# Expert gate and up in one TensorE core: rows held and split weights streamed in three fp32r products, with down one block behind

## What is computed

```python
MOE_BLOCK = 128
def run_block(args):
    xb, e = args                                   # 128 rows of 1024, the block's expert
    hid = jax.nn.silu(xb @ w_gate[e]) * (xb @ w_up[e])   # 1024 x 512 each
    return hid @ w_down[e]                         # 512 x 1024
yb = lax.map(run_block, (buf.reshape(n_blocks, MOE_BLOCK, D), block_e)).reshape(n_rows, D)
```

## Time and profile before

| | us |
|---|---|
| median of 3 runs | 3437.43 |
| lowest and highest run | 3433.58, 3445.54 |
| the profiled execution's own time | 3432.71 |
| its span, first to last instruction | 3431.0 |
| TensorE busy in the span | 2979.0 (87%) |
| VectorE, ScalarE, GpSimd busy | 1231.0, 1004.2, 233.1 |
| mean granted TensorE clock | 0.901 of full |

### The profile page before, as it was taken

How to read it: one execution, slowest core, us unless ns; L and a number is a source line. 1 busy time by engine, 2 the same in 40 slices (tenths; PEclk the granted TensorE clock), 3 DMA queues, 4 the chain that set the end, 5 groups by cost and what they waited for, 6 DMA issues and landing times. The chain is left out here.

```text
span 3431.0 us, 41076 instructions
## 1 busy us (share of the span) xinstructions
PE 2979.0 (87%) x15738; PEld 2379.3 (69%) x15738; DVE 1231.0 (36%) x2668; ACT 1004.2 (29%) x1633; POOL 233.1 (7%) x281
## 2 busy tenths in 40 slices
PE   5999799896499999995599989999698878888877
PEld 4887566596499999995478857788697734444457
DVE  4444411222233333334412135333222224555542
ACT  4223211111133333332411112112222324444431
POOL 0000300000200000002001012201100000000000
PEclk9999899996699999998799979558799888999989
DMA  3110641121599999996433144112203100000021
GB/s 84 43 46 4 256 142 38 36 75 58 205 345 342 344 344 344 344 343 232 145 98 117 43 132 97 51 28 50 96 13 98 33 19 1 1 1 1 1 86 68
DMA packets 284590, 412.06 MB, mean 120 GB/s; under 512 B 73579, under 2 KB 167403, under 8 KB 284332
## 3 DMA queue, kind: packets, MB, share of 16 engines
q1 hardware_dynamic: 247328, 302.70, 27.2%
q0 software_dynamic: 21088, 73.42, 5.6%
q10 hardware_dynamic: 16044, 34.17, 2.7%
HBM read 334.89 MB, written 75.28 MB: 120 GB/s over the span
## 5 line engine op out<-in xcount | busy, mean ns | idle before, releaser
L1280 PE MATMUL ps<-moe_xT,moe_wg 128*128 128x128 f32 x2048 | 251.3, 276 | 1.0 <-DVE moe_xT L1328 1.0
L1280 PE MATMUL ps<-moe_xT,moe_wu 128*128 128x128 f32 x2048 | 249.8, 275 | 0.0
L1280 PEld LDWEIGHTS ps<-moe_xT,moe_wg 128*128 128x128 f32 x2048 | 242.9, 193 | 4.0 <-issue 1.4
L1280 PEld LDWEIGHTS ps<-moe_xT,moe_wu 128*128 128x128 f32 x2048 | 239.3, 192 | 0.0
L155 DVE TENSOR_TENSOR moe_wd_parts<-moe_wd,moe_wd_parts 128x1024 fp32r<-128x1024 f32 x128 | 148.5, 1220 | 114.1 <-ACT moe_wd_parts L1309 114.1
L1937 PE MATMUL ps<-att_qx,att_kx 65*128 65x256 f32 (+1 forms) x512 | 165.4, 465 | 7.0 <-DMA att_qx<-att_RR 7.0
L2442 PE MATMUL ps<-c_kT,c_q 96*128 96x512 f32 (+3 forms) x384 | 153.1, 508 | 1.2 <-ACT c_kT L2489 0.7
L2020 ACT ACTIVATE att_sT<-att_sT 128x512 f32<-128x512 f32 (+1 forms) x104 | 63.8, 614 | 286.9 <-DVE att_sT L2095 286.9
L2463 PE MATMUL ps<-lattn_pT,X 128*64 128x512 f32 (+3 forms) x384 | 144.2, 531 | 0.7 <-ACT lattn_pT L2516 0.7
L1937 PEld LDWEIGHTS ps<-att_qx,att_kx 65*128 65x128 f32 x512 | 124.4, 285 | 20.7 <-DMA att_qx<-att_RR 7.1
L148 PE MATMUL ps<-ab_h,abp_w 128*128 128x512 f32 x336 | 134.9, 401 | 3.5 <-DVE abp_w L155 3.5
(11 more groups left out here) (470 smaller groups left out, 6343.1 us busy)
## 6 DMA issues: line engine op xcount, KB each, us to landing
moe_wg<-in_w_e_gate_dram SPq DMA_DIRECT2D x128, 512.0 KB, 4.8
moe_wu<-in_w_e_up_dram SPq DMA_DIRECT2D x128, 512.0 KB, 4.7
moe_wd<-in_w_e_down_dram SPq DMA_DIRECT2D x128, 512.0 KB, 9.3
y_rows<-merge_zero POOLq DMA_DIRECT2D x49, 512.0 KB
y_rows<-moe_y ACTq DMA_DIRECT2D x32, 512.0 KB, 5.5
abp_raw<-in_ab_w_in_dram SPq DMA_DIRECT2D x22, 512.0 KB, 4.1
proj_w_raw<-in_w_in_dram SPq DMA_DIRECT2D x20, 512.0 KB, 4.1
merge_raw<-in_w_in_dram SPq DMA_DIRECT2D x16, 512.0 KB, 6.7
```

The source lines that it names most:

```text
L1280: mm = pe.matmul(ps[:, which, f * P:(f + 1) * P], w[:, k, f * P:(f + 1) * P], xT[:, k, :], start=(k == 0 and f == 0), stop=(k == KT - 1), ...
```

## The change

Gate, up and down all become three fp32r products with the rows (or hidden rows) stationary, and 512 columns of weights streamed. The result of gate and up then has the rows on the partitions, so the hidden rows have to be turned on TensorE ahead of down (`turn_hidden`), and the turned rows and turned hidden rows are split into high and low parts. All weights are split: ScalarE copies the landed chunk to a high tile, and VectorE writes the low part over the landed chunk itself (`split_tile` puts the raw and the low tile at one address). GpSimd makes two of the four low parts of down. A chunk's next load therefore waits until TensorE has used the chunk. Down of block j runs after gate and up of block j + 1; the first and last turns are written out ahead of the loop and behind it. Gate and up chunks are cut from memory in another way: a partition takes eight consecutive weight rows, two to a chunk, so each chunk reads 4 KB in every 16 KB; before, a chunk was 512 KB in one piece, in rows of 2 KB.

```diff
-                link(dve.tensor_copy(R["n_blocks"][:, :], pend[0:1, cur, EXPERTS - 1:EXPERTS]))
+                for i in range(3):
+                    link(dve.tensor_scalar(be[:, i:i + 1], pend[0:1, cur, EXPERTS - 1:EXPERTS], -float(i), None, ALU.add))
+                link(dve.tensor_copy(R["n_blocks"][:, :], be[:, 0:3]))
...
+        def split_tile(name, shape):
+            high, at = sc.sb(name + "_high", shape, F32R), aligned(nc.sbuf_base)
+            low = sc.sb(name + "_low", shape, F32R)
+            return high, low, nc.alloc_sbuf_tensor_at(f"moe_{name}_raw", shape, F32, offset=at)
...
-        wg_d = w_gate.rearrange("e (c k p) f -> (e c) p k f", p=P, k=2)
+        wg_d = w_gate.rearrange("e (p c k) f -> e p c (k f)", c=GC, k=2)
+        wu_d = w_up.rearrange("e (p c k) f -> e p c (k f)", c=GC, k=2)
+        wd_d = w_down.rearrange("e (c p) d -> e p c d", p=P)
+        xg_cols = xg[:, :].rearrange("t (p k) -> t k p", k=KT)
...
+                def load_down(b, e):
                     for f in range(FT):
-                        sp.wait_ge(wd_split, i * FT + f + 1)
+                        sp.wait_ge(d_used, b * FT + (f + 1))
...
+                with sp.Fori(0, loops) as j:
+                    e = expert_of(j + 2)
+                    load_gate(j + 2, e)
+                    load_up(j + 2, e)
+                    load_down(j + 1, expert_of(j + 1))
...
+                def low_down(b):
+                    for i in range(ON_POOL):
+                        f = FT - ON_POOL + i
+                        pool.wait_ge(d_high, b * FT + (f + 1))
+                        pool.tensor_tensor(wd[1][:, f, :], wd[2][:, f, :], wd[0][:, f, :].bitcast(F32), ALU.subtract).then_inc(d_split_pool, 1)
+                with pool.Fori(0, loops) as j:
+                    gather(j + 3)
+                    low_down(j + 1)
...
+                def gate_up(b, bank, w, split, used):
                     for c in range(GC):
-                        for which, w in enumerate((wg, wu)):
-                            pe.wait_ge(loaded[2 * c + which], i * 16 + 16)
-                                    mm = pe.matmul(ps[:, which, f * P:(f + 1) * P], w[:, k, f * P:(f + 1) * P], xT[:, k, :],
+                        pe.wait_ge(split, b * GC + (c + 1))
+                        for k in range(2):
+                            n = 2 * c + k
+                            mm = multiply_split(pe, ps[:, bank, :], (xT[:, 0, n, :], xT[:, 1, n, :]), (w[0][:, c, k, :], w[1][:, c, k, :]), n == 0, n == KT - 1)
+                        mm.then_inc(used, 1)
...
+                with pe.Fori(0, loops) as j:
+                    gate(j + 1)
+                    turn_hidden(j)
+                    up(j + 1)
+                    turn_x(j + 2)
+                    down(j)
...
+                def high(b, w, loaded, made, c):
+                    act.wait_ge(loaded[c], b * 16 + 16)
+                    act.activation(w[0][:, c], w[2][:, c], ACT.Copy).then_inc(made, 1)
+                def rows_high(b):
+                    act.wait_ge(x_turned, b + 2)
+                    act.wait_ge(u_used, b * GC + GC)
+                    for n in range(2):
+                        act.activation(xT[:, 0, 4 * n:4 * n + 4, :], ps[:, 4 + n, :].rearrange("p (k t) -> p k t", t=P), ACT.Copy).then_inc(x_high, 1)
...
+                def low(b, w, n, high, made, c):
+                    dve.wait_ge(high, b * n + (c + 1))
+                    low_part(dve, w[1][:, c], w[2][:, c], w[0][:, c]).then_inc(made, 1)
```

More of the change, by code:

```diff
@@ L1222, in experts @@
+        hT = sc.sb("hT", [P, 2, FT, P], F32R)
         y = sc.sb("y", [P, D])
[L1223 to L1226 removed]
@@ L1264, in _ @@
+                last, loops = blocks_less(pool, 1), blocks_less(pool, 2)
+                for b in range(3):
+                    gather(b)
+                low_down(0)
+                with pool.Fori(0, loops) as j:
+                    gather(j + 3)
+                    low_down(j + 1)
+                low_down(last)
             @block.tensor
             def _(pe):
[L1266 to L1269, removed]
@@ L1320, in _ @@
-                act.wait_ge(y_stored, nb * 16 + 16)
+                last, loops = blocks_less(act, 1), blocks_less(act, 2)
+                rows_high(0)
+                for c in range(GC):
+                    high(0, wg, g_loaded, g_high, c)
+                for c in range(GC):
+                    high(0, wu, u_loaded, u_high, c)
+                silu(0)
+                for c in range(GC):
+                    high(1, wg, g_loaded, g_high, c)
+                for c in range(GC):
+                    high(1, wu, u_loaded, u_high, c)
@@ new lines, in _ @@
+                rows_high(1)
+                for f in range(FT):
+                    high(0, wd, d_loaded, d_high, f)
+                with act.Fori(0, loops) as j:
+                    silu(j + 1)
+                    for c in range(GC):
+                        high(j + 2, wg, g_loaded, g_high, c)
+                    hidden_high(j)
+                    for c in range(GC):
+                        high(j + 2, wu, u_loaded, u_high, c)
+                    rows_high(j + 2)
+                    for f in range(FT):
+                        high(j + 1, wd, d_loaded, d_high, f)
+                    out(j)
@@ L1321, in _ @@
+                silu(last)
+                hidden_high(loops)
+                for f in range(FT):
+                    high(last, wd, d_loaded, d_high, f)
+                out(loops)
+                hidden_high(last)
+                out(last)
+                act.wait_ge(y_stored, last * 16 + 32)
                 act.sem_inc(settled_act, 1)
@@ new lines, in out @@
+                def out(b):
+                    dve.wait_ge(d_used, b * FT + 2 * FT)
+                    dve.wait_ge(y_stored, b * 16 + 16)
+                    dve.tensor_copy(y[:, HALF:D], ps[:, 3, :]).then_inc(y_dve, 1)
+                dve.sem_inc(y_dve, 1)
+                dve.sem_inc(x_low, 2)
+                dve.sem_inc(hid_ready, 1)
+                dve.sem_inc(h_low, 1)
+                last, loops = blocks_less(dve, 1), blocks_less(dve, 2)
+                rows_low(0)
+                for c in range(GC):
+                    low(0, wg, GC, g_high, g_split, c)
@@ new lines, in _ @@
+                for c in range(GC):
+                    low(0, wu, GC, u_high, u_split, c)
+                for c in range(GC):
+                    low(1, wg, GC, g_high, g_split, c)
+                hidden(0)
+                for c in range(GC):
+                    low(1, wu, GC, u_high, u_split, c)
+                rows_low(1)
+                for f in range(FT - ON_POOL):
+                    low(0, wd, FT, d_high, d_split, f)
+                with dve.Fori(0, loops) as j:
+                    for c in range(GC):
+                        low(j + 2, wg, GC, g_high, g_split, c)
+                    hidden_low(j)
+                    hidden(j + 1)
+                    for c in range(GC):
+                        low(j + 2, wu, GC, u_high, u_split, c)
+                    rows_low(j + 2)
+                    for f in range(FT - ON_POOL):
+                        low(j + 1, wd, FT, d_high, d_split, f)
+                    out(j)
@@ L1351, in combine @@
+                hidden_low(loops)
+                hidden(last)
+                for f in range(FT - ON_POOL):
+                    low(last, wd, FT, d_high, d_split, f)
+                out(loops)
+                hidden_low(last)
+                out(last)
 def combine(nc, K, R, y_dram):
```

203 lines of the change are left out of this document (113 added, 90 removed).

## The result

The changed kernel took 3500.14 us (median of 4 runs, 3482.21 to 3518.79), the kernel before 3435.51 (4 runs) beside it: ratio 1.0169, 95% interval 1.012 to 1.0218. It is slower by some 65 us, where 3405 was forecast, and outside the range. The profiled execution took 3502.45; all of what follows is read from it.

A forecast was written before the change was run, and what follows sets the result against it. Rings of waits through the single-buffered weight tiles, L + 15.3 with L = 4.7, were to set a 20.0 us period; the stage ends at 1559.0 instead of 1591.9, 32.9 us off 3437.4, so 3405 us, range 3368 to 3455.

The forecast's parts named there:

- TensorE's work: Expert stage: gate, up and down at 5.46 us each plus turning 0.91 and 0.46, 17.75 us a block against 21.33.
- The DMA floor: Expert stage: 7.34 MB a block moved at an assumed 400 GB/s, so at least 18.4 us a block.
- The second ring: From down's last product through its last chunk's load and ScalarE's list to the next down: L + 15.30 us.
- L: Time from a weight load's issue to its landing, taken as 4.7 us.
- which then waits twice a block, some 2.2 us in all: TensorE waits before gate for the rows' low part and before down for the hidden rows', some 2.2 us a block.
- TensorE whose clock falls because it pauses: Slower case in the expert stage, sharing a chance of 0.04 with a ring beyond 5.8 + 0.3.
- Two rings close over one block: Expert stage: one ring through the rows, one through ScalarE's list, both L + 15.3, giving a period of 20.0 us.
- down's ring: The second ring, through down's last chunk and ScalarE's list: L + 15.30 us.
- the ring through the rows: From up's last product through its last chunk, the rows' low parts, gate, turning and up: L + 15.25 us.
- break-even: Period of 21.1 us, or L = 5.8, at which the change gains nothing; rival of no change, chance 0.15.
- Slow pieces: Rival: gate and up loads, 4 KB pieces 16 KB apart, run slowly; at 320 GB/s 3492 us; chance 0.11.
- VectorE and GpSimd block each other: Rival: their low parts can't run together, delaying up to 2.36 us a block; period 22.4, time 3476; chance 0.07.

The follow-up runs named there:

- The fastest run: Changed kernel with a raw tile of its own for every weight chunk and hidden and input rows' parts moved ahead of the splits: 3351.4 us, ratio 0.9779.
- the run with the input parts earlier: Changed kernel with only the input rows' high and low parts moved ahead of the splits of up: 3495.0 us, ratio 1.018.
- the hidden parts earlier: Changed kernel with the turned hidden rows' copy and low part moved ahead of gate's four chunk copies and low parts: 3496.0 us, ratio 1.0193.

## Why the prediction was wrong

- **TensorE's work, 17.75 us a block: right.** With nothing in its way a block takes 17.9, TensorE busy 98.9% of it.
- **The DMA floor, 18.4 us at 400 GB/s: near, and a little too high.** The fastest run moves 410 GB/s over 300 us and has a period of 17.89, under that floor. The Trainium skill's 358 GB/s ("DMA: Bandwidth & Descriptors", Specifications) was the other reading; this run does not hold to it, with one core active.
- **The second ring, L + 15.30 with L = 4.7: the right ring, mis-sized.** In the block shown L is 5.33 (+0.63), down 7.24 in place of 5.46 (+1.78, of which 1.55 is the clock), the four low parts of gate 4.96 to the start of the next in place of 4.64 (+0.32); 20.0 + 2.73 = 22.73, and 22.77 was measured. Over the stage, the second gate ends at 945.62 and the last one at 1625.21 (each read at the start of the turning behind it): 30 periods of 22.65 in place of 20.0, 79.6 us more. With 8.7 at the start (945.6 against 936.9) and 6.0 at the end, that is the 94 us by which the stage ended later than forecast. Another 8 us of the profiled execution stand behind the stage, where nothing was changed.
- **The first step that failed: "which then waits twice a block, some 2.2 us in all".** The wait was seen, and given no price beyond itself. Behind 2.9 us of pause the products of down ran at the granted 0.50 for 3 us, on the ring that the prediction had as one of the two longest. A "TensorE whose clock falls because it pauses" had a part of 0.04 in the chances. Without the clock's 1.55 this ring would have come to 21.2, which is what the run with the input parts earlier shows in its blocks with the clock at 1.00.
- **The second: "Two rings close over one block": three do.** The ring through gate's last chunk, L + 15.8, is longer than either, 20.5 at my own L of 4.7, 21.6 at gate's median of 5.8 and 22.8 at the 7.06 that its last chunk took once the pause was filled. It is why filling the pause in the changed kernel gave back 0.26 us of 1.55. Either step alone would have been enough for the loss: down's ring with the clock comes to 22.7 without the third one, and with the clock at 1.00 the period was still 22.39. Without both, down's ring at 21.2 and the ring through the rows at 21.7 (L + 15.25 with up's median of 6.4) stand at or over the 21.1 that the prediction has as its break-even, so L and the products' price alone would have taken the gain.
- **L = 4.7: too low.** The medians over the stage are 5.8 for gate, 6.4 for up and 4.7 for down. That down's agrees is no support, for the ring needs the last chunk of a block, and down's chunks take longer from first to last: from issue to copy 3.8, 4.7, 5.3 and 5.2 us as medians of the window. "None queues behind another for long" did not hold: gate's and up's loads are issued in step with TensorE, and in the shown block the whole core moved 233 GB/s from 1206.4 to 1209.4. Loads were late there and not slow: nothing had been freed to load. Just before, from 1200.0 to 1204.9, it had moved 416 GB/s at a share of 1.02, so the loads come in bursts. What sets the rest of L was not settled.
- **Slow pieces: wrong,** and shown so by two runs.
- **VectorE and GpSimd block each other: the mechanism was there, at 0.36 us a block** and not 2.36. The Trainium skill's rule that such operations of the two engines contend ("SBUF — State Buffer", Who interferes with whom) agrees in kind.

Shown by runs are that the pause lowers the clock and what that costs where down's ring stands alone, the two engines' part, that the pieces cost nothing, and that several rings of nearly equal length hold the period. That the loss of one block splits into 1.78, 0.63 and 0.32 is read from one trace; since the rings take over from one another, none of the three can be had back at its price by itself.

## What to carry over

When single buffers tie loads to their use, list every ring through every buffer, and not the first two that fit; where several are within a microsecond or two, only an edit that shortens all of them pays, and an edit tried alone says nothing against it. On in-order engines the cheap cut is the order: a small part that TensorE waits for goes ahead of a run of long splits. Put into a ring the landing of the chunk that closes it, and not the median of all chunks. Price a pause of TensorE with the lower clock behind it, above all where the products behind it lie on the ring.

## Not expected of the hardware

- One core moved 410 GB/s over 300 us with 4 KB pieces and a DMA share of 1.02, where the same pieces gave 324 at 0.91 and the kernel before 344 at 0.95. A share near 0.95 did not mean that the rate was near its limit.
- The landing of down's 512 KB grew from 4.7 us at 324 GB/s to 6.7 at 394 while the kernel got faster. The mean rate alone does not set it: with the hidden parts earlier it was 6.3 at 330.
- The granted clock did not fall at one fixed point, nor after every pause. In the block shown it fell 1.4 us after TensorE had started again. Before the block at 1159.01 it fell within the pause of 3.00 us, as the line below shows. In the run with the input parts earlier, 11 of the 26 pauses (2.3 to 3.3 us each) were followed by no fall in down at all.

```profile
1158.00:1159.00 1.00, 0.00 (x0) 0.00 (x0) 1.00 (x3) 0.81 (x2) 1.00 (x1) 0.61 0.97 397
```
